# Pair 4 of the input projection between the steps of the sample indexer scores

## The chip, the cores and the metric

The kernel runs on one core of a Trainium2 chip. The metric is the device time of one execution in microseconds (us); several executions are taken and their median counts. The profile is of one execution, with its own time.

## What is computed

One layer of a hybrid decoder, for 256 prompt tokens and 8 x 4 = 32 sample tokens that share all weights. Cut to what matters here:

```python
p = rmsnorm(x) @ w_in                       # 2048 -> q, k, v, qi (16 heads x 64), ki, wi, conv and gate parts
# indexer of the sample tokens, over 2048 cached positions of each of 8 sequences (and 4 new ones)
s = relu(einsum('bthd,bsd->bths', qi, ki)) * 64**-0.5
score = einsum('bths,bth->bts', s, wi * 16**-0.5)
_, idx = top_k(score, 256)                  # per sample token
# attention over the 256 picked cache rows
out = sparse_attend(q, cache_k[page, off(idx)], cache_v[page, off(idx)])
x = x + (sigmoid(ga) * (out @ w_pa) + sigmoid(gb) * (conv @ w_pb)) @ w_o
x = x + relu(rmsnorm(x) @ w1)**2 @ w2       # 2048 -> 8192 -> 2048
```

## The kernel before, in words

All products with large weights are made in three fp32r matmuls each (high x high, high x low, low x high). `w_in` is cut into 44 pairs of 256 output columns; `win_half(p, half)` (L393) does half a pair, which is four *eighths*. An eighth is 12 matmuls of 288 columns and one `chunk_used` increment. Eighths are counted through: eighth u = 8 p + j, so pair 4 is eighths 32 to 39. For every eighth, SyncE loads the raw weights, ScalarE (ACT) makes the high part `VH` (`highs`, L881), and GpSimd (POOL) or, for some eighths from pair 16 on, VectorE (DVE) the low part `VL` (POOL's `lows`, L1706). `VH` and `VL` are rings of four, so ACT makes `VH` of eighth u when eighth u - 4 has been used, and the matmuls wait for `VL` (`low_done`). Pair p accumulates in PSUM banks 0 and 1 (even p) or 2 and 3 (odd p), and ACT's `evac` copies it out.

Every engine runs its own list of instructions, in the order that the program writes. Semaphores alone tie the lists together.

The helper `after` of `win_half` is called behind each eighth, and small work of PE is put there: while pairs 2 and 3 run, the prompt's indexer scores (`prompt_scores`, L551). The sample's indexer scores stand behind pair 3 as one block, with no eighth in it (L611 to L638). For sequence b:

- `turn_keys(b)` (L579): 8 transposes of cached index keys into banks 6 and 7; it waits for DVE's copies of two steps before (`kp_copied`).
- DVE's `keys(b)` (L1313) copies them to `kiP`.
- `scores(b)` (L591): 4 products of the queries with 512 keys each, into banks 0 and 1 for even b, 4 and 5 for odd b. ACT takes the ReLU of each bank (L988).
- `combine(b)` (L604): weights the 16 heads and sums them into banks 2 and 3, in 2 products. Each line of the profile counts these fp32 products twice.

Behind `combine(7)` ACT and DVE copy the scores to SBUF (L1345, `scomb_added`). PE waits for that, then does pairs 4 to 7. DVE goes on with the sample's top-k: 32 rounds of max, index and replace (L1361 to L1364), a merge of two halves up to `comb_ready` (L1381), and two steps of the prompt's own top-k (`prompt_top`, L1387). PE waits for `comb_ready` in `picked(0)`, behind the first eighth of pair 14 (L655 to L660), and spreads the positions. DVE works out the cache rows from these (L1396 to L1404, `rows_ready`).

POOL does `lows` of all eighths below 120, then waits for `rows_ready`:

```python
            lows(UNIT * KP)                      # KP = 15, UNIT = 8
            pool.wait_ge(S["rows_ready"], 1)
            for n in range(UNITS + RK):
                lows(UNIT * KP + n if n < RK else unit_end(n - RK) + 4)
                gather(n)
```

So each low part from eighth 120 on stands behind a gather of cache rows in POOL's list. DVE works on the gathered rows, one unit after another (L1433, L1438), and at n = 4 waits for PE's products of pair 16 (L684; DVE L1448).

Of the kernel before, what the change touches and what calls it, by code (L numbers as in the profile page):

```python
# [6 lines left out]
ACT = mybir.ActivationFunctionType  # L7
# [108 lines left out]
def build(nc, I, O):  # L116
    with ExitStack() as ctx:
# [267 lines left out]
        def _(pe):  # L385
# [165 lines left out]
            def prompt_scores(h):  # L551
                if h % 4 == 0:
                    pe.wait_ge(S["win_evac"], h // 4 + 1)
                if h == 0:
                    pe.wait_ge(S["kin_copied"], 2)
                    pe.wait_ge(S["wc_copied"], 1)
                else:
                    pe.wait_ge(S["pscore_relu"], h)
                for a, n in ((0, P), (P, SEQ)):
                    for e in range(2):  # L560
                        r = ID * e
                        m = pe.matmul(bank(5 - e, a, n), qiT[r:r + ID, h // 2, a % SEQ:a + P], kiT[r:r + ID, 0:n], start=True, stop=True)
                        if a:
                            m.then_inc(S["pscore_done"], 1)
# [14 lines left out]
            def turn_keys(b):  # L579
                pe.wait_ge(pages_in[b], 16)  # L580
                for c in range(2):
                    at = 2 * b + c
                    if at < 2:
                        pe.wait_ge(S["tab_copied"], H - 1 + at)
                    else:
                        pe.wait_ge(S["kp_copied"], at - 1)
                    for g in range(4):
                        m = transpose(bank(6 + c, g * P, P), rawk[b][:, 4 * c + g, :])
                    m.then_inc(S["kp_turned"], 1)

            def scores(b):  # L591

                pe.wait_ge(S["kp_copied"], 2 * b + 2)
                if b >= 2:
                    pe.wait_ge(S["sscore_relu"], 2 * b - 2)
                q = qs2[:, b].rearrange("p h t -> p (h t)")
                for c in range(2):
                    for e in range(2):
                        r, o = ID * e, ID * (e ^ c)
                        m = pe.matmul(PM[o:o + ID, 4 * (b % 2) + c, :], q[r:r + ID, :], kiP[r:r + ID, b % 2, 512 * c:512 * c + 512],  # L600
                                      start=True, stop=True)
                    m.then_inc(S["sscore_done"], 1)

            def combine(b):  # L604

                pe.wait_ge(S["sscore_relu"], 2 * b + 2)
                for c in range(2):
                    m = pe.matmul(PM[ID * c:ID * c + ID, 2 + c, :], Wc[:, b, :], rl[:, b % 2, c, :], start=(b == 0), stop=(b == DB - 1))
                m.then_inc(S["scomb_done"], 1)

            turn_keys(0)  # L611
            prompt_scores(12)
            prompt_scores(14)
            turn_keys(1)
            pe.wait_ge(S["wc_copied"], 1)
            pe.wait_ge(S["qs_copied"], 4)
            pe.wait_ge(S["pscore_relu"], IH)
            for b in range(DB):
                scores(b)
                if b == 0:  # L620
                    for i in range(DB):
                        m = pe.matmul(bank(3, DT * i, DT, ID), qs2[0:ID, i].rearrange("p h t -> p (h t)"),
                                      kiT[0:ID, SEQ + DT * i:SEQ + DT * i + DT], start=True, stop=True)
                    m.then_inc(S["snew_done"], 1)
                if b + 2 < DB:
                    turn_keys(b + 2)
                if b:
                    combine(b - 1)
            pe.wait_ge(S["snew_relu"], 1)
            for i in range(DB):  # L630
                m = pe.matmul(bank(3, ID, DT, NS), Wc[0:ID, i, 0:NS], rln[:, DT * i:DT * i + DT], start=(i == 0), stop=(i == DB - 1))
            m.then_inc(S["snew_done"], 1)
            combine(DB - 1)
            pe.wait_ge(S["consts_in"], 16)
            pe.wait_ge(S["ptf_ready"], 1)
            pe.wait_ge(S["kp_copied"], 2 * DB)
            pe.matmul(bank(5, 0, NPG), const("rall", NS), ptf[:], start=True, stop=True).then_inc(S["spread_done"], 1)
            pe.wait_ge(S["scomb_added"], 4)  # L638

            pairs(4, 8)  # L640
            win_half(8, 0)
            pe.wait_ge(S["win_evac"], 8)
            pe.wait_ge(S["ptw_read"], 1)
# [200 lines left out]
        def _(act):  # L844
# [137 lines left out]
                act.wait_ge(tabs[i], 32)  # L982
            for at in range(2 * DB):
                b, c = at // 2, at % 2
                act.wait_ge(S["sscore_done"], at + 1)
                if b >= 2:
                    act.wait_ge(S["scomb_done"], b - 1)
                act.activation(rl[:, b % 2, c, :], bank(4 * (b % 2) + c), ACT.Relu).then_inc(S["sscore_relu"], 1)  # L988
                if at == 1:
                    act.wait_ge(S["snew_done"], 1)  # L990
                    act.activation(rln, bank(3, 0, NS, ID), ACT.Relu).then_inc(S["snew_relu"], 1)
# [872 lines left out]
```

## Time and profile before

| | |
|---|---|
| median of 3 runs | 1791.46 us (1788.7 to 1793.67) |
| the profiled execution's own time | 1791.65 us |
| its span | 1789.9 us |
| PE, DVE, ACT, POOL busy | 1751.0, 1039.0, 690.1, 563.9 us |

Busy shares are means over stages. PE's matmuls overlap, so an eighth of 12 matmuls, each listed with some 0.3 us, starts a matmul every 0.13 us and takes 1.6 us. The timelines give starts in microseconds from the start of the span. An idle time stands in brackets with what ended it. PEclk is the granted TensorE clock as a share of the full one.

### The profile page before, as it was taken

To read this page: it belongs to the slowest core of one execution; us is meant where nothing else is said; L and a number is where in the kernel's file an instruction comes from. 1 tells how busy PE (TensorE), PEld (TensorE's weight loads), DVE (VectorE), ACT (ScalarE), POOL (GpSimd) and SP (SyncE) were. 2 spreads that over 40 slices of the span, in tenths; PEclk is the share of its full clock that TensorE was granted. 3 is DMA by queue.
4 is the path that set the end of the run, shared out by engine and by line. 5 is a ranking of instruction groups with operands and counts; after the bars stand their busy time and mean duration, and the time that the engine had idled before them with its cause. 6 is when DMAs were issued, how large, how long until landed. Compare 5 with 4: busy or idle time off the path is not lost.

```text
span 1789.9 us, 32474 instructions
## 1 busy us (share of the span) xinstructions
PE 1751.0 (98%) x13712; PEld 1701.0 (95%) x13712; DVE 1039.0 (58%) x1147; ACT 690.1 (39%) x845; POOL 563.9 (32%) x450
## 2 busy tenths in 40 slices
PE   9999999999999999999999999999999999999997
PEld 8859998999888999999999999999999999999996
DVE  4559997889989432255456554455444554455543
ACT  5534443543344555433333332233323332233332
POOL 3718778888866667400231000000000000000001
PEclk9999999999999999999999999999999999999998
DMA  6725457988879974654454444444444444444442
GB/s 211 239 66 156 153 166 256 349 296 295 306 263 316 337 275 152 209 182 159 167 187 156 165 164 165 164 165 163 166 163 165 164 164 165 164 165 164 163 165 100
DMA packets 73793, 348.53 MB, mean 195 GB/s; under 512 B 8978, under 2 KB 11154, under 8 KB 52660
## 3 DMA queue, kind: packets, MB, share of 16 engines
q1 hardware_dynamic: 50112, 268.00, 44.0%
q0 software_dynamic: 19584, 71.31, 11.4%
q10 hardware_dynamic: 3988, 7.66, 1.2%
q8 instruction: 81, 1.33, 0.3%
q14 instruction: 28, 0.23, 0.0%
HBM read 340.50 MB, written 6.44 MB: 194 GB/s over the span
## 4 chain that ended last, share of the span: by engine, by line
PE 86%; DVE 10%; POOL 2%; DMA 1%; issue 1%; ACT 0%; POOLq 0%; DVEq 0%; ACTq 0%
PE PM L426 19%; PE PM L428 19%; PE PM L427 19%; PE PM L406 8%; PE PM L408 7%; PE PM L407 7%; PE PM L391 2%; DVE lg L1438 2%; DVE kv L1433 2%; DVE VL L1428 2%; PE PM L783 1%; DMA kv<-cache_v,offs 1%; POOL VL L1712 1%; POOL kv L1726 1%; DVE sp L1498 1%
## 5 line engine op out<-in xcount | busy, mean ns | idle before, releaser
L849 ACT ACTIVATE WH<-wring 128x2048 fp32r<-128x2048 f32 (+1 forms) x163 | 307.3, 1885 | 679.9 <-PE PM L428 676.1
L1582 DVE TENSOR_TENSOR WL<-wring,WH 128x2048 fp32r<-128x2048 f32 x159 | 364.5, 2292 | 341.3 <-ACT WH L849 341.2
L406 PE MATMUL PM<-hH,VH 128*128 128x288 f32 x1408 | 428.9, 305 | 11.1 <-POOL VL L1712 6.9
L1712 POOL TENSOR_TENSOR VL<-wring,VH 128x512 fp32r<-128x512 f32 x292 | 383.4, 1320 | 163.5 <-ACT VH L849 147.8
L407 PE MATMUL PM<-hL,VH 128*128 128x288 f32 x1408 | 418.7, 297 | 0.0
L408 PE MATMUL PM<-hH,VL 128*128 128x288 f32 x1408 | 417.3, 296 | 0.0
L426 PE MATMUL PM<-XH,WH 128*128 128x288 f32 x1280 | 379.1, 296 | 1.5 <-DVE WL L1589 1.5
L426 PE MATMUL PM<-YH,WH 128*128 128x288 f32 x1280 | 379.4, 296 | 0.0
L427 PE MATMUL PM<-YL,WH 128*128 128x288 f32 x1280 | 377.6, 295 | 0.0
L427 PE MATMUL PM<-XL,WH 128*128 128x288 f32 x1280 | 377.6, 295 | 0.0
L428 PE MATMUL PM<-XH,WL 128*128 128x288 f32 x1280 | 376.3, 294 | 0.0
L428 PE MATMUL PM<-YH,WL 128*128 128x288 f32 x1280 | 376.3, 294 | 0.0
L849 ACT ACTIVATE VH<-wring 128x512 fp32r<-128x512 f32 x352 | 221.7, 631 | 336.7 <-PE PM L408 336.2
L406 PEld LDWEIGHTS PM<-hH,VH 128*128 128x128 f32 x1408 | 267.2, 190 | 24.6 <-POOL VL L1712 8.9
L408 PEld LDWEIGHTS PM<-hH,VL 128*128 128x128 f32 x1408 | 268.2, 190 | 0.0
L407 PEld LDWEIGHTS PM<-hL,VH 128*128 128x128 f32 x1408 | 267.6, 190 | 0.2
L1767 POOL TENSOR_SCALAR ysam<-ysam,small 32x1024 f32<-32x1024 f32 x2 | 6.2, 3122 | 824.1 <-DVE small L1688 824.1
L426 PEld LDWEIGHTS PM<-XH,WH 128*128 128x128 f32 x1280 | 239.8, 187 | 1.8 <-ACT G L926 1.7
L428 PEld LDWEIGHTS PM<-XH,WL 128*128 128x128 f32 x1280 | 241.0, 188 | 0.0
L428 PEld LDWEIGHTS PM<-YH,WL 128*128 128x128 f32 x1280 | 241.0, 188 | 0.0
L427 PEld LDWEIGHTS PM<-XL,WH 128*128 128x128 f32 x1280 | 240.2, 188 | 0.1
L427 PEld LDWEIGHTS PM<-YL,WH 128*128 128x128 f32 x1280 | 240.2, 188 | 0.0
(267 smaller groups left out, 1574.4 us busy)
## 6 DMA issues: line engine op xcount, KB each, us to landing
wring<-w_in SPq DMA_DIRECT2D x176, 512.0 KB, 4.6
wring<-w_mlp_in SPq DMA_DIRECT2D x64, 1024.0 KB, 5.2
wring<-w_mlp_out SPq DMA_DIRECT2D x64, 1024.0 KB, 5.2
wring<-w_o SPq DMA_DIRECT2D x16, 1024.0 KB, 5.2
wring<-w_pb SPq DMA_DIRECT2D x8, 1024.0 KB, 4.9
wring<-w_pa SPq DMA_DIRECT2D x8, 1024.0 KB
xT<-x_t SPq DMA_DIRECT2D x1, 2304.0 KB, 12.2
bias_scratch<-uv ACTq DMA_DIRECT2D x8, 192.0 KB, 4.6
```

Source lines behind the costliest of these rows:

```text
L391: return pe.transpose(out, in_, cp[0:n, 0:n])
L406: pe.matmul(out, vh, hH[:, k, :], start=(k == 0), stop=False)
L407: pe.matmul(out, vh, hL[:, k, :], start=False, stop=False)
L408: m = pe.matmul(out, vl, hH[:, k, :], start=False, stop=(k == KT - 1))
L426: pe.matmul(out, wh, rh[:, k0 + k, :], start=(first and k == 0), stop=False)
L427: pe.matmul(out, wh, rl_[:, k0 + k, :], start=False, stop=False)
L428: m = pe.matmul(out, wl, rh[:, k0 + k, :], start=False, stop=(last and k == CK - 1))
L849: return act.activation(out, in_, ACT.Copy, **kw)
L1428: dve.tensor_tensor(VL[:, u % 4], r, VH[:, u % 4], ALU.subtract).then_inc(S["vl_dve"], 1)
L1433: m = dve.tensor_tensor(by2, by2, PM[:, 6:8, :], ALU.mult)
L1582: dve.tensor_tensor(WL[:, i % 2], wring[:, i % 2], WH[:, i % 2], ALU.subtract).then_inc(S["wl_ready"], 1)
L1712: pool.tensor_tensor(VL[:, u % 4], r, VH[:, u % 4], ALU.subtract).then_inc(S["vl_pool"], 1)
```

## The change

The block of the sample scores is cut into four parts, and each is put behind one of the first four eighths of pair 4, by way of `after`. `turn_keys(0)` and `prompt_scores(12)` stay ahead of pair 4. Then:

- eighth 32, then `prompt_scores(14)` and `turn_keys(1)`
- eighth 33, then sequence 0's scores, `turn_keys(2)`, and the products with the new keys
- eighth 34, then the whole steps of sequences 1 to 7, and the new keys' weighting
- eighth 35, then `combine(7)` and the spread of the page table; then eighths 36 to 39

The wait for `scomb_added` now stands behind pair 4. Pair 4 needs banks 0 and 1, so all sample scores use banks 4 and 5, and scores of sequence b wait, for each of the two banks, for the ReLU of sequence b - 1. ACT makes `VH` of eighths 36, 37 and 38 between the ReLUs.

```diff
--- before.py
+++ after.py
@@ -591,13 +591,13 @@
             def scores(b):
 
                 pe.wait_ge(S["kp_copied"], 2 * b + 2)
-                if b >= 2:
-                    pe.wait_ge(S["sscore_relu"], 2 * b - 2)
                 q = qs2[:, b].rearrange("p h t -> p (h t)")
                 for c in range(2):
+                    if b:
+                        pe.wait_ge(S["sscore_relu"], 2 * b - 1 + c)
                     for e in range(2):
                         r, o = ID * e, ID * (e ^ c)
-                        m = pe.matmul(PM[o:o + ID, 4 * (b % 2) + c, :], q[r:r + ID, :], kiP[r:r + ID, b % 2, 512 * c:512 * c + 512],
+                        m = pe.matmul(PM[o:o + ID, 4 + c, :], q[r:r + ID, :], kiP[r:r + ID, b % 2, 512 * c:512 * c + 512],
                                       start=True, stop=True)
                     m.then_inc(S["sscore_done"], 1)
 
@@ -608,36 +608,47 @@
                     m = pe.matmul(PM[ID * c:ID * c + ID, 2 + c, :], Wc[:, b, :], rl[:, b % 2, c, :], start=(b == 0), stop=(b == DB - 1))
                 m.then_inc(S["scomb_done"], 1)
 
-            turn_keys(0)
-            prompt_scores(12)
-            prompt_scores(14)
-            turn_keys(1)
-            pe.wait_ge(S["wc_copied"], 1)
-            pe.wait_ge(S["qs_copied"], 4)
-            pe.wait_ge(S["pscore_relu"], IH)
-            for b in range(DB):
+            def ask(b):
+
                 scores(b)
-                if b == 0:
+                if b + 2 < DB:
+                    turn_keys(b + 2)
+                if b:
+                    combine(b - 1)
+
+            def samples(j):
+                if j == 0:
+                    prompt_scores(14)
+                    turn_keys(1)
+                    pe.wait_ge(S["wc_copied"], 1)
+                    pe.wait_ge(S["qs_copied"], 4)
+                    pe.wait_ge(S["pscore_relu"], IH)
+                elif j == 1:
+                    ask(0)
                     for i in range(DB):
                         m = pe.matmul(bank(3, DT * i, DT, ID), qs2[0:ID, i].rearrange("p h t -> p (h t)"),
                                       kiT[0:ID, SEQ + DT * i:SEQ + DT * i + DT], start=True, stop=True)
                     m.then_inc(S["snew_done"], 1)
-                if b + 2 < DB:
-                    turn_keys(b + 2)
-                if b:
-                    combine(b - 1)
-            pe.wait_ge(S["snew_relu"], 1)
-            for i in range(DB):
-                m = pe.matmul(bank(3, ID, DT, NS), Wc[0:ID, i, 0:NS], rln[:, DT * i:DT * i + DT], start=(i == 0), stop=(i == DB - 1))
-            m.then_inc(S["snew_done"], 1)
-            combine(DB - 1)
-            pe.wait_ge(S["consts_in"], 16)
-            pe.wait_ge(S["ptf_ready"], 1)
-            pe.wait_ge(S["kp_copied"], 2 * DB)
-            pe.matmul(bank(5, 0, NPG), const("rall", NS), ptf[:], start=True, stop=True).then_inc(S["spread_done"], 1)
+                elif j == 2:
+                    for b in range(1, DB):
+                        ask(b)
+                    pe.wait_ge(S["snew_relu"], 1)
+                    for i in range(DB):
+                        m = pe.matmul(bank(3, ID, DT, NS), Wc[0:ID, i, 0:NS], rln[:, DT * i:DT * i + DT], start=(i == 0), stop=(i == DB - 1))
+                    m.then_inc(S["snew_done"], 1)
+                else:
+                    combine(DB - 1)
+                    pe.wait_ge(S["consts_in"], 16)
+                    pe.wait_ge(S["ptf_ready"], 1)
+                    pe.wait_ge(S["kp_copied"], 2 * DB)
+                    pe.matmul(bank(5, 0, NPG), const("rall", NS), ptf[:], start=True, stop=True).then_inc(S["spread_done"], 1)
+
+            turn_keys(0)
+            prompt_scores(12)
+            win_half(4, 0, samples)
+            win_half(4, 1)
             pe.wait_ge(S["scomb_added"], 4)
-
-            pairs(4, 8)
+            pairs(5, 8)
             win_half(8, 0)
             pe.wait_ge(S["win_evac"], 8)
             pe.wait_ge(S["ptw_read"], 1)
@@ -982,10 +993,12 @@
                 act.wait_ge(tabs[i], 32)
             for at in range(2 * DB):
                 b, c = at // 2, at % 2
+                if at in (2, 4, 6):
+                    highs(UNIT * 4 + 4 + at // 2)
                 act.wait_ge(S["sscore_done"], at + 1)
                 if b >= 2:
                     act.wait_ge(S["scomb_done"], b - 1)
-                act.activation(rl[:, b % 2, c, :], bank(4 * (b % 2) + c), ACT.Relu).then_inc(S["sscore_relu"], 1)
+                act.activation(rl[:, b % 2, c, :], bank(4 + c), ACT.Relu).then_inc(S["sscore_relu"], 1)
                 if at == 1:
                     act.wait_ge(S["snew_done"], 1)
                     act.activation(rln, bank(3, 0, NS, ID), ACT.Relu).then_inc(S["snew_relu"], 1)
```

## Rows read from the trace of the kernel before

**Rows 1.** The page's first part: engine, busy us (share of the span), instructions.

```profile
PE 1751.0 (98%) x13712; PEld 1701.0 (95%) x13712; DVE 1039.0 (58%) x1147; ACT 690.1 (39%) x845; POOL 563.9 (32%) x450
```

**Rows 2.** Stretches: busy us of PE, PEld, DVE, ACT, POOL; granted clock, DMA share, GB/s.

```profile
96.00:132.00 36.00, 31.61 (x225) 15.15 (x224) 19.57 (x43) 13.13 (x26) 2.24 (x2) 0.95 0.11 30
132.00:262.00 130.00, 130.00 (x967) 128.46 (x966) 126.38 (x176) 55.75 (x90) 100.66 (x79) 1.00 0.52 162
410.00:420.00 10.00, 6.69 (x30) 6.46 (x30) 9.86 (x10) 1.26 (x2) 7.84 (x7) 0.66 0.67 222
```

**Rows 3.** PE's timeline: start, us, engine, line, operation, count, [idle before <-releaser].

```profile
88.78 0.40 PE L406 MATMUL PM<-hH,VH 128*128 128x288 f32 x1
...
92.17 0.93 PE L562 MATMUL PM<-kiT,G 64*128 64x128 f32 x8
...
98.83 0.93 PE L562 MATMUL PM<-kiT,G 64*128 64x128 f32 x8 [0.47 <-ACT G L926]
100.71 0.93 PE L562 MATMUL PM<-kiT,G 64*128 64x128 f32 x8 [0.95 <-ACT rlp L959]
...
103.67 1.04 PE L622 MATMUL PM<-kiT,qs 64*64 64x4 f32 x16
106.06 1.91 PE L391 MATMUL PM<-cp,kv 128*128 128x128 f32 x8 [1.34 <-DVE zB L1319]
...
109.69 1.09 PE L391 MATMUL PM<-cp,kv 128*128 128x128 f32 x8
...
112.74 1.09 PE L391 MATMUL PM<-cp,G 128*128 128x128 f32 x8
...
127.98 0.66 PE L631 MATMUL PM<-uv,zB 64*32 64x4 f32 x16
128.58 1.08 PE L608 MATMUL PM<-uv,zB 128*64 128x512 f32 x4
...
131.50 0.40 PE L406 MATMUL PM<-hH,VH 128*128 128x288 f32 x1 [1.52 <-DVE small L1350]
```

**Rows 4.** ACT's timeline, a ReLU pair of the sample scores.

```profile
112.84 1.09 ACT L988 ACTIVATE uv<-PM 128x512 f32<-128x512 f32 x2 [1.96 <-PE PM L600]
```

**Rows 5.** POOL's timeline, the low part of pair 4's fourth eighth.

```profile
97.28 1.27 POOL L1712 TENSOR_TENSOR VL<-wring,VH 128x512 fp32r<-128x512 f32 x1 [0.32 <-ACT VH L849]
```

**Rows 6.** DVE's timeline, around the sample top-k.

```profile
129.77 1.41 DVE L1345 COPY scw<-PM 32x512 f32<-32x512 f32 x2 [5.90 <-PE PM L608]
...
260.93 0.41 DVE L1381 TENSOR_TENSOR comb<-PM,scw 32x256 f32<-32x256 f32 x1
...
265.53 0.23 DVE L1396 TENSOR_SCALAR small<-PM 128x64 f32<-128x64 f32 x1 [0.91 <-PE PM L659]
```

**Rows 7.** PE's timeline at the picked positions.

```profile
264.25 1.18 PE L659 MATMUL PM<-comb,cp 32*128 32x64 f32 x8
265.35 0.40 PE L406 MATMUL PM<-hH,VH 128*128 128x288 f32 x1
```

**Rows 8.** POOL's timeline where its gathers begin.

```profile
268.02 4.62 POOL L1712 TENSOR_TENSOR VL<-wring,VH 128x512 fp32r<-128x512 f32 x3 [1.62 <-ACT VH L849]
272.96 0.95 POOL L1726 DMA_INDIRECT kv<-cache_k,offs  x1 [0.32 <-DVE offs L1404]
...
280.56 2.83 POOL L1726 DMA_INDIRECT kv<-cache_k,offs  x1 [0.16 <-issue]
```

**Rows 9.** DVE's timeline, the compare beside those gathers and the next wait on PE.

```profile
278.62 3.94 DVE L1417 TENSOR_TENSOR scw<-dist,cp 128x2048 f32<-128x2048 f32 x1
...
303.40 0.16 DVE L1448 TENSOR_SCALAR newsel<-PM 128x1 f32<-128x1 f32 x1 [8.33 <-PE PM L684]
```

**Rows 10.** PE's timeline, two of its waits for POOL behind the gathers.

```profile
284.73 0.40 PE L406 MATMUL PM<-hH,VH 128*128 128x288 f32 x1 [2.42 <-POOL VL L1712]
...
293.25 0.40 PE L406 MATMUL PM<-hH,VH 128*128 128x288 f32 x1 [0.22 <-POOL VL L1712]
```

**Rows 11.** PE's timeline, a longer wait for POOL in the unit loop.

```profile
414.08 0.61 PE L406 MATMUL PM<-hH,VH 128*128 128x288 f32 x1 [3.31 <-POOL VL L1712]
```

## The prediction

> **What bounds the kernel now.** I read the page's busy shares first. PE is busy for 1751.0 of 1789.9 us [rows 1], so the natural guess is that every microsecond saved on PE is a microsecond of the end. The stretches correct that. In 96:132, the block of sample scores, PE is busy for only 31.61 of 36 us, at a clock of 0.95. In 132:262 PE has no idle time, but DVE is busy for 126.38 of 130 us too [rows 2]: two engines run side by side there, and which of them arrives last at their meeting has to be read from the timelines. The reader is to look in these for brackets, which are idle time with its releaser.
>
> PE's timeline of the block shows four losses [rows 3]. PE waits 0.95 us for the ReLUs of prompt scores ahead of 100.71, 1.34 us for DVE's key copy ahead of 106.06, and 1.52 us for DVE's score copies ahead of 131.50. The fourth is clock: behind the wait of 1.34 us, transposes take 1.91 us where the same eight take 1.09 us at 109.69. From 106.06 to 109.69 PE does two thirds of a step (transposes, scores) in 3.63 us. A whole step of three equal parts takes 3.05 us (109.69 to 112.74), two thirds 2.03, so the half clock costs 1.6 us. The sum of what could be filled is 0.95 + 1.34 + 1.6 + 1.52 = 5.4 us.
>
> DVE's timeline shows the other side. DVE waits 5.90 us for PE's last combine and starts on the copies at 129.77. From there its list is a chain of dependent steps up to the merge that ends at 260.93 + 0.41 = 261.34 (`comb_ready`) [rows 6]. PE comes to the picked positions at 264.25 [rows 7]: DVE has 2.9 us in hand at this meeting. DVE fills them with its prompt top-k until 264.62, then waits 0.91 us for PE and goes on at 265.53 [rows 6]. POOL's first gather at 272.96 is released by DVE's cache rows [rows 8], and PE waits for POOL's low parts behind the gathers, 2.42 us at 284.73 and 0.22 us at 293.25 [rows 10].
>
> **The change, PE's side.** Without a break PE starts 967 matmuls in 130 us [rows 2], 0.134 us each, so an eighth of 12 takes 1.6 us. Two eighths between small work take 92.17 - 88.78 = 3.4 us [rows 3], so entry and exit together cost 0.2, and a single eighth costs 1.8 us. PE's list from `prompt_scores(12)` on becomes: eighth 32 covers the wait of 0.95, eighths 32 and 33 put `turn_keys(2)` at 98.83 + 0.9 + 1.8 + 0.9 + 1.0 + 1.8 + 1.0 = 106.2 (scores, eighth, scores, transposes, eighth, sequence 0's scores), which is past the 106.06 at which DVE's copy is there. The order of the new keys' products (1.04 us at 103.67) and `turn_keys(2)` is swapped, which costs nothing by that sum. With no long idle stretch I take the clock as full, as it is in all other steps of the block. The 1.52 us go behind pair 4, where DVE's two copies of together 1.41 us have four eighths, 6.4 us, to be done in. PE gains 5.4 less four more pairs of seams, 4 x 0.2 = 0.8, so 4.6 us. The low parts of the four eighths are ready: POOL finishes the fourth at 98.55 [rows 5]. If these weren't hidden, each would cost 1.3 us, its duration.
>
> **The change, two banks.** A pair of ReLUs starts at 112.84, which is 1.12 us behind its scores' start (two thirds of a step behind 109.69), and ends 2.2 us behind it, the first 1.65 us behind it [rows 3, 4]. The next scores of that bank come a step later, 3.05 us, and in the last step, which has no transposes, 2.03 and 2.54 us for the two banks. All are later than the ReLUs; the narrowest slack is 0.3 us. ACT's three high parts stand between ReLU pairs, where ACT waits 1.96 us each time; a high part of 0.63 us fits. Cost nothing; from the other side, if each of the seven steps waited for one high part, 7 x 0.6 = 4 us.
>
> **The change, DVE's side.** This decides. `combine(7)` now stands behind four eighths that it did not stand behind before. It ends later by 4 x 1.80 = 7.2 less the losses filled ahead of it, 0.95 + 1.34 + 1.6 = 3.9: by 3.3 us. DVE's whole chain starts 3.3 us later, and `comb_ready` comes at 261.34 + 3.3 = 264.6. PE would be there at 264.25 - 4.6 = 259.65 and waits 5.0 us. PE's gain is gone at one blow: it goes on at 264.7, 0.45 us later than before. DVE does its prompt steps until 264.62 + 3.3 = 267.9, by which PE's positions (1.1 us, 2.2 at half clock) are there, so it no longer waits 0.91 us: 267.9 against 265.53, 2.4 us later. The cache rows, and with them POOL's first gather, are 2.4 us later. PE then meets POOL. The eighth that starts at 284.73 is number 123, ten behind the one at 265.35 [rows 7]. Without a wait PE would start it at 265.35 + 0.45 + 10 x 1.61 = 281.9, but POOL's low part moves with the gathers, and with it the start, to 287.1. So PE is 2.4 us late there too and at 293.25. Behind that nothing resynchronises: DVE waits 8.33 us for PE at 303.40 [rows 9], so it starts its units 2.4 us later, and PE, DVE, POOL all carry the shift to the end. I find no place where one of them has work that did not shift.
>
> **Bounds of the shift.** A wait of 5.0 us is longer than any shown. Behind 3.31 us at 414.08 the first matmul takes 0.61 instead of 0.40 us [rows 11], and 410:420 has a clock of 0.66, 6.8 us of ten at the half level [rows 2]; behind 1.34 us the half level lasted 3.6 us. So PE probably loses 1.8 to 3.4 us behind the positions. That is covered by the 5.2 us between 281.9 and 287.1. It can still delay POOL: its last low parts end at 272.64, 0.32 us ahead of the gather [rows 8]; moved by 0.45 + 3.4 they end at 276.5, 1.4 us later than the cache rows (275.1). Upper end 2.4 + 1.4 = 3.8 us. The fourth gather, though, takes 2.83 us instead of 0.95, and ends at 283.39, 0.8 us behind DVE's compare of 278.62 + 3.94 [rows 8, 9]; if the compare holds it, POOL's lateness is absorbed there. I take 2.4. Lower end: if the drop at 106 stays in spite of the filling, DVE is 1.6 us later still and PE gains less, which is again on the upper side; if the seams cost nothing, 1.6.
>
> The Trainium skill speaks against the pinning: "SBUF — State Buffer", section "Who interferes with whom", says that a DVE instruction with two SBUF inputs contends with a GpSimd instruction that reads SBUF and not with one that only writes it, and infers that descriptor generation needs the write side. By that rule the gather would pass the compare, and the sum would be 2.4 to 3.8; by the row of 2.83 us it is 2.4.
>
> **Rivals.** First, the gain holds: PE is the bound, DVE has room, and the end is 4.6 us earlier, 1791.46 - 4.6 = 1786.9. For it: PE's share of 98%, and no PE idle time in 132:262. Against it: the 2.9 us of slack are less than the 3.3 by which DVE starts later, and the later waits for POOL hang on DVE. It needs DVE's list to be no chain, or a later wait of DVE for PE that sets the end.
>
> Second, clearly slower, by the clock: the wait of 5.0 us at 259.65 is followed by the low level, and the waits ahead of the eighth of 287.1 by another fall, which lies behind POOL's last gate at 295.6 and is not covered. It decides as soon as the second low stretch reaches past 295.6. Price 1.8 to 3.4 us on 2.4 to 3.8: 1795.7 to 1798.7. For it: a fall stood behind 1.34 us of idle time. Against it: behind 2.42 us the matmul at 284.73 takes 0.40 us, and so does the one at 293.25 [rows 10], against 0.61 at the low level.
>
> The skill, in "TensorE: Matmul & The Clock Gate", section "HAM oscillation — how this bites in real kernels", says that a long wait between bursts sends the engine back to half clock and that each burst then starts slowly. The fall behind 3.31 us agrees; by this rule the new wait of 5.0 us does the same, and by the rows its cover holds.
>
> Third, two banks are too few and every step waits, 4 us on PE and on DVE's start: 1791.5 + 2.4 + 4 = 1797.9.
>
> **Numbers.** The profiled execution took 1791.65 us, 1.75 more than its span of 1789.9 and 0.2 more than the median of the runs. The shift put on the median gives 1791.46 + 2.4 = 1793.9; I say 1794. The chances: this account 0.68, the gain holds 0.08, the clock 0.17, the banks 0.07. What can be told from no change is about 0.3%, 5.4 us, so below 1786.1 or above 1796.8. Faster by that needs the first rival and more, 0.04; slower is half of the clock's cases, most of the banks', and a tail of the forecast, 0.16; the same is 0.80. The forecast's own range is 1791 to 1797. For 8 in 10, with the runs before spread over 5 us, I give 1788.5 to 1798.5.
>
> **What would show it.** Right: no PE bracket of 1.34 or 1.52 us near 106 and 131; a full clock in the steps; `combine(7)` 3 us later; eighth 36 without a wait; a new wait of PE of some 5 us ahead of L659 with DVE's L1381 as releaser; DVE's 0.91 us ahead of L1396 gone; the first gather at 275 to 276; the eighth of 284.73 near 287; everything behind 293 shifted by the same amount. Wrong: no wait at L659, or PE brackets of half a microsecond ahead of each L600, or DVE's units starting earlier than at 303.4.

## The result: slower by 0.47%, beyond the upper end of the range

The changed kernel takes 1798.87 us (median of 6 runs, 1798.39 to 1803.62), the kernel before 1790.88 us (6 runs). The ratio is 1.0047, 95% interval [1.0035, 1.0059]. The forecast was 1794, the range 1788.5 to 1798.5. The shift has the sign of the forecast and about three times its size (8.0 us by the medians, 2.4 forecast). The wait that the forecast named is there, but the first gather is not released by what it named. The case "within 0.3%", which had 0.80, is not what came.

Spans and busy times of the profiled execution (1798.39 us) come first; the line answers to [rows 1].

```profile
PE 1754.3 (98%) x13712; PEld 1703.9 (95%) x13712; DVE 1041.4 (58%) x1147; ACT 690.2 (38%) x845; POOL 564.6 (31%) x450
```

The stretches of the changed kernel answer to [rows 2]: busy time of PE, PEld, DVE, ACT, POOL, then clock, DMA share and GB/s.

```profile
96.00:132.00 36.00, 35.39 (x264) 19.97 (x263) 18.41 (x36) 14.22 (x28) 6.11 (x5) 1.00 0.13 41
132.00:262.00 130.00, 127.84 (x944) 125.13 (x942) 125.23 (x167) 56.26 (x91) 100.40 (x78) 1.00 0.53 163
266.00:275.00 9.00, 8.51 (x39) 8.39 (x40) 8.46 (x23) 1.21 (x2) 1.55 (x1) 0.56 0.01 3
310.00:320.00 10.00, 10.00 (x58) 10.00 (x58) 9.42 (x9) 1.92 (x4) 5.58 (x5) 0.66 0.74 250
```

The block of the sample scores is what it was meant to be: PE is busy for 35.39 of 36 us at full clock. But 132:262 now has idle time on PE, and 266:275 runs at a clock of 0.56. PE's timeline answers to [rows 3, 7, 10, 11].

```profile
105.34 1.09 PE L600 MATMUL PM<-zB,qs 64*64 64x512 f32 x8
106.36 1.09 PE L391 MATMUL PM<-cp,kv 128*128 128x128 f32 x8
107.38 1.09 PE L629 MATMUL PM<-kiT,qs 64*64 64x4 f32 x16
...
110.19 1.09 PE L600 MATMUL PM<-zB,qs 64*64 64x512 f32 x8
...
132.10 1.08 PE L608 MATMUL PM<-uv,zB 128*64 128x512 f32 x4
133.11 0.39 PE L644 MATMUL PM<-ptf,cp 32*128 32x16 f32 x2
...
266.49 1.96 PE L670 MATMUL PM<-comb,cp 32*128 32x64 f32 x8 [6.65 <-DVE comb L1394]
268.38 0.61 PE L406 MATMUL PM<-hH,VH 128*128 128x288 f32 x1
...
290.52 0.40 PE L406 MATMUL PM<-hH,VH 128*128 128x288 f32 x1 [0.56 <-POOL VL L1725]
...
299.03 0.40 PE L406 MATMUL PM<-hH,VH 128*128 128x288 f32 x1 [0.21 <-POOL VL L1725]
...
421.44 0.61 PE L406 MATMUL PM<-hH,VH 128*128 128x288 f32 x1 [3.31 <-POOL VL L1725]
```

None of the three waits of [rows 3] behind 98.83 is left, and no transposes at half clock. `combine(7)` starts at 132.10 instead of 128.58, 3.5 us later. PE then waits 6.65 us for DVE ahead of L670 (before: L659), and its products take 1.96 us instead of 1.18. At 299.03 PE is 5.8 us late against 293.25, at 421.44 it is 7.4 us late against 414.08.

DVE's timeline answers to [rows 6, 9], POOL's to [rows 8].

```profile
133.30 1.41 DVE L1358 COPY scw<-PM 32x512 f32<-32x512 f32 x2 [7.89 <-PE PM L608]
134.63 1.25 DVE L1362 TENSOR_SCALAR small<-cp 32x4 f32<-32x4 f32 x1
135.92 0.15 DVE L1363 TENSOR_TENSOR small<-PM,cp 32x4 f32<-32x4 f32 x1
136.10 1.29 DVE L1365 TENSOR_TENSOR small<-small 32x4 f32<-32x4 f32 x1
...
137.90 1.21 DVE L1374 MAX8 scw<-scw 64x8 f32<-64x1026 f32 x1
...
266.02 0.41 DVE L1394 TENSOR_TENSOR comb<-PM,scw 32x256 f32<-32x256 f32 x1
...
269.75 0.22 DVE L1409 TENSOR_SCALAR small<-PM 128x64 f32<-128x64 f32 x1
...
274.14 0.23 DVE L1416 SCALAR_TENSOR_TENSOR small<-dist,small 128x64 f32<-128x64 f32 x1
274.40 0.20 DVE L1417 CAST offs<-small 128x64 uint32<-128x64 f32 x1
...
281.21 2.29 DVE L1430 TENSOR_TENSOR scw<-dist,cp 128x2048 f32<-128x2048 f32 x1
```
```profile
134.57 1.29 POOL L1725 TENSOR_TENSOR VL<-wring,VH 128x512 fp32r<-128x512 f32 x1 [17.26 <-ACT VH L860]
136.09 1.29 POOL L1725 TENSOR_TENSOR VL<-wring,VH 128x512 fp32r<-128x512 f32 x1 [0.23 <-ACT VH L860]
...
275.14 3.58 POOL L1725 TENSOR_TENSOR VL<-wring,VH 128x512 fp32r<-128x512 f32 x2 [1.15 <-ACT VH L860]
278.87 0.95 POOL L1739 DMA_INDIRECT kv<-cache_k,offs  x1 [0.15 <-issue]
...
281.30 3.03 POOL L1739 DMA_INDIRECT kv<-cache_k,offs  x1 [0.16 <-issue]
...
288.21 0.95 POOL L1739 DMA_INDIRECT kv<-cache_k,offs  x1 [0.16 <-issue]
```

For comparison, the same short steps of DVE in the kernel before, POOL's first low part behind the block, and DVE's last two steps to the cache rows:

```profile
131.11 0.15 DVE L1349 TENSOR_SCALAR small<-cp 32x4 f32<-32x4 f32 x1
131.29 0.15 DVE L1350 TENSOR_TENSOR small<-PM,cp 32x4 f32<-32x4 f32 x1
131.48 0.15 DVE L1352 TENSOR_TENSOR small<-small 32x4 f32<-32x4 f32 x1
```
```profile
134.16 1.29 POOL L1712 TENSOR_TENSOR VL<-wring,VH 128x512 fp32r<-128x512 f32 x1 [35.61 <-ACT VH L849]
```
```profile
270.25 1.20 DVE L1403 SCALAR_TENSOR_TENSOR small<-dist,small 128x64 f32<-128x64 f32 x1
271.49 1.19 DVE L1404 CAST offs<-small 128x64 uint32<-128x64 f32 x1
```

Three things stand here that the forecast did not have.

- Two steps of DVE behind the score copies take 1.25 and 1.29 us, where the one between them takes 0.15 us as all three did; both lie under a low part of POOL (134.57 and 136.09, 1.29 us each).
- DVE's cache rows are there at 274.60, but the first gather goes out at 278.87: POOL was still at two low parts, 275.14 to 278.72. Its bracket says "issue", not DVE.
- DVE does L1409 4.2 us later than L1396 before, but its cache rows come only 1.9 us later (274.60 against 272.68). In the kernel before, the last two steps took 1.20 and 1.19 us beside POOL's low parts; here POOL is idle then and they take 0.23 and 0.20 us. So of the first gather's 5.9 us, DVE's lateness makes 1.9.

### The profile page after: what moved, and what is told of

Read it like the earlier page. It is cut to its first block, busy times and chain, and to the rows that moved or that the text cites. A ratio compares the mean times of both kernels' runs of the same rounds, so it can differ in the third digit from the quotient of the medians.

```text
span 1796.6 us, 32475 instructions
## 1 busy us (share of the span) xinstructions
PE 1754.3 (98%) x13712; PEld 1703.9 (95%) x13712; DVE 1041.4 (58%) x1147; ACT 690.2 (38%) x845; POOL 564.6 (31%) x450
## 4 chain that ended last, share of the span: by engine, by line
PE 80%; DVE 16%; POOL 2%; DMA 1%; issue 1%; ACT 1%; POOLq 0%; ACTq 0%; DVEq 0%
PE PM L426 19%; PE PM L428 19%; PE PM L427 19%; PE PM L406 6%; PE PM L408 5%; PE PM L407 5%; DVE ix L1375 2%; DVE scw L1377 2%; DVE scw L1374 2%; PE PM L391 2%; DVE lg L1451 2%; DVE kv L1446 2%; DVE VL L1441 1%; PE PM L794 1%; POOL VL L1725 1%
## 5 line engine op out<-in xcount | busy, mean ns | idle before, releaser
L1725 POOL TENSOR_TENSOR VL<-wring,VH 128x512 fp32r<-128x512 f32 x292 | 383.2, 1319 | 172.2 <-ACT VH L860 155.4
```

The costliest lines, as they stand in the source:

```text
L1725: pool.tensor_tensor(VL[:, u % 4], r, VH[:, u % 4], ALU.subtract).then_inc(S["vl_pool"], 1)
```

## The experiments

Profiles differ by up to 3.4 us ahead of the changed part; in 16:45 the granted clock was 0.88 in some (before, after) and 0.76 in others (e1, e3). So times are given here from the start of `prompt_scores(12)` in the same profile (98.83 before, 98.87 after). L659, L1396 and L684 are the lines of the kernel before; the same instructions have other line numbers in the changed ones. Ratios are against runs of the kernel before on the same chip.

| | score copies | top-k starts | L659 | L1396 | first gather | L684 | ratio, 95% interval |
|---|---|---|---|---|---|---|---|
| before | 30.9 | 33.3 | 165.4 | 166.7 | 174.1 | 203.5 | 1 |
| after | 34.4 | 39.0 | 167.6 | 170.9 | 180.0 | 209.2 | 1.0047 [1.0035, 1.0059] |
| e1_picked_late | 34.4 | 39.0 | 167.7 | 170.9 | 176.0 | 205.3 | 1.0021 [1.0011, 1.0031] |
| e2_keep_warm | 34.5 | 39.1 | 167.7 | 170.9 | 178.1 | 207.4 | 1.0022 [1.0012, 1.0031] |
| e3_two_eighths | 30.8 | 33.1 | 162.4 | 165.7 | 172.8 | 202.4 | 1.0006 [0.9997, 1.0016] |
| e4_two_banks | 31.2 | 33.5 | 165.6 | 166.9 | 174.4 | 203.7 | 1.0007 [0.9997, 1.0017] |
| e5_quiet_start | 34.4 | 36.8 | 167.3 | 169.3 | 174.4 | 203.8 | 1.0004 [0.9993, 1.0014] |
| e6_two_tops_later | 30.8 | 33.1 | 162.4 | 163.6 | 169.8 | 199.4 | 0.9985 [0.9975, 0.9996] |
| e7_dve_delayed | 34.3 | 36.7 | 171.0 | 172.3 | 179.7 | 209.2 | 1.0047 [1.0031, 1.0062] |
| e8_tops_later | 30.7 | 33.1 | 165.2 | 166.4 | 173.9 | 203.2 | 0.9998 [0.9988, 1.0007] |
| e9_chain_late_3 | 31.0 | 40.1 | 169.0 | 172.2 | 179.8 | 210.0 | 1.0040 [1.0028, 1.0053] |
| e10_chain_late_8 | 30.9 | 52.9 | 181.0 | 184.3 | 193.4 | 222.7 | 1.0107 [1.0090, 1.0124] |
| e11_quiet_only | 34.4 | 36.8 | 166.0 | 169.3 | 176.8 | 206.8 | 1.0026 [1.0015, 1.0036] |
| e12_four_tops_later | 34.5 | 36.8 | 167.3 | 168.5 | 173.7 | 203.1 | 1.0002 [0.9992, 1.0012] |

Two readings hold for all rows. From the first gather to L684 every profile takes 29.2 to 30.1 us: what the first gather is late by, L684 is late by, within a microsecond. Behind L684 chance comes in. The clock falls beside the small products of L688 in some profiles and not in others, and from L688 to the next transposes of `kT` it takes 6.9 us with no fall (e5, e9, e11), 8.4 us with 3.4 us at the low level (before, e2, e4, e8), and 10.0 us with 6.8 us (the rest). No edit was made to change that. The profiled execution of e9 took 1796.05 us and four of its six took 1799.05 to 1800.38, so it seems to differ between executions of one kernel too; no second profile of a kernel shows it. Up to 3 us of a difference between two rows can be this fall.

**The wait and the clock: e1 and e2.**

```diff
-            win_half(KP - 1, 0, picked)
-            win_half(KP - 1, 1)
+            win_half(KP - 1, 0)
+            win_half(KP - 1, 1, picked)
```

> The changed kernel, with the products at the picked positions (L670) moved from behind the first eighth of pair 14 to behind its fifth, four eighths later (6.4 us of PE work ahead of the wait). Theory A (the wait of 6.65 us ahead of L670 lowers TensorE's clock to half until 274.8, so eighths 113 to 119, POOL's low parts behind them and POOL's first gather come late): the wait shrinks to under 1 us, no low clock in 262:276, the first gather comes at 275 to 277 instead of 278.9, and the kernel takes 1795 to 1797 us. Theory B (only DVE's own chain, 5.1 us late at L1394, sets the end): the first gather stays at 278.9 and the time at 1799 us. Prediction's account with only sizes off: as A.

Measured: 1796.23 us. PE does its four eighths ahead of the wait, which is 0.28 us instead of 6.65; 262:276 is at full clock (in the changed kernel the low level ends at 274.0, not at 274.8); the first gather waits for DVE's rows again and comes 4.0 us earlier. By the ratios that is 0.26% or 4.7 us of the loss of 0.47%. PE and POOL in e1:

```profile
269.92 1.17 PE L670 MATMUL PM<-comb,cp 32*128 32x64 f32 x8 [0.28 <-DVE comb L1394]
...
280.99 0.58 PE L406 MATMUL PM<-hH,VH 128*128 128x288 f32 x1 [4.91 <-POOL VL L1725]
```
```profile
278.30 0.95 POOL L1739 DMA_INDIRECT kv<-cache_k,offs  x1 [8.18 <-DVE offs L1417]
```

PE's lead is still worth nothing: it is idle for 4.91 us ahead of 280.99, at the first low part behind a gather. The clock falls there instead (6.8 us at the low level in 279:287), but PE is paced by the gathers in that stretch, and L684 follows the first gather by 29.3 us as elsewhere.

```diff
                 if j == 0:
+                    pe.wait_ge(S["win_evac"], KP - 1)
+                    for i in range(26):
+                        pe.matmul(bank(2, 0, P), ones[:], ones[:], start=True, stop=True)
                     pe.wait_ge(S["comb_ready"], 1)
```

> The changed kernel, with 26 idle products of the ones tile (128 columns, fp32, about 6 us) ahead of the wait for comb_ready, so that PE is busy while it waits. Nothing else moves. Theory A (the clock after the wait): full clock in 266:276, L670 at 266.5 as before the edit, eighth 113 to 119 in 11.3 us instead of 15, first gather at 275 to 276.5, time 1794.5 to 1796.5 us. Theory B (DVE's lateness alone): L670 at 266.5 and 1799 us all the same.

Measured: 1795.9 us. L659 starts at the same time as in the changed kernel, and the stretch 262:276 has these values (PE busy, clock, DMA share, GB/s):

```profile
262.00:276.00 14.00, 13.15 (x104) 1.00 0.22 74
```

The clock behind the wait is what this edit changes, and its ratio is that of e1 (1.0022 and 1.0021). The first gather gains less (1.9 us) since POOL now works beside DVE's steps to the rows: DVE's 128x1024 products take 2.26 and 2.20 us there, 1.23 in the changed kernel. The shorter fall behind L684 (3.4 us instead of 6.8 at the low level in the profile) may be the rest of the gain. The theory of the wait and the clock holds, that of DVE's lateness alone does not: with L659 as late as in the changed kernel, the gather is earlier.

**The short steps under POOL: e5 and e11.**

```diff
+            act.wait_ge(S["ptw_read"], 1)
             for p in range(4, 8):
                 evac(p, qT[:, 2 * (p - 4):2 * (p - 4) + 2, :])
```

ACT's high parts from eighth 39 on, and with them POOL's low parts, now wait until DVE has done its short steps. In e5 this stands beside the edit of e1, in e11 alone.

> The changed kernel with the picked positions behind the fifth eighth of pair 14 (as in e1_picked_late), and ACT's next high parts (eighth 39 on) held back until DVE's short steps behind combine(7) are done (ACT waits for ptw_read). Theory C (in the changed kernel POOL's low parts at 134.57 and 136.09 hold DVE's short steps of 0.15 us for 1.25 and 1.29 us, so the top-k starts 2.2 us later than combine(7) makes it): those two steps take 0.15 us again, the top-k starts 3.6 us behind the start of the score copies' line less 1.4 (2.4 us behind it instead of 4.6), comb_ready is 2.2 us earlier relative to the score copies, and the kernel is 1 to 2.2 us faster than e1_picked_late (1796.2). Rival: the short steps are slow for another reason and nothing moves; 1796 us.

> The changed kernel, with only ACT's high parts from eighth 39 on held back until DVE's short steps are done; the picked positions stay behind the first eighth of pair 14. With the changed kernel, e1_picked_late and e5_quiet_start it makes a two by two of the two causes. Short steps 0.15 us each, comb_ready 1.6 to 2.2 us earlier than in the changed kernel, but a wait of about 5 us at L659 remains, the clock falls, POOL's low parts are late as they were. If the causes add: 1.5 to 2.2 us faster than the changed kernel, 1797 us. If the clock alone sets the first gather: no faster than by the shorter wait, 1797 to 1799 us.

Measured: 1791.84 us (e5) and 1795.31 us (e11). DVE and POOL in e5:

```profile
134.48 1.41 DVE L1359 COPY scw<-PM 32x512 f32<-32x512 f32 x2 [7.90 <-PE PM L608]
135.82 0.15 DVE L1363 TENSOR_SCALAR small<-cp 32x4 f32<-32x4 f32 x1
136.00 0.15 DVE L1364 TENSOR_TENSOR small<-PM,cp 32x4 f32<-32x4 f32 x1
136.19 0.15 DVE L1366 TENSOR_TENSOR small<-small 32x4 f32<-32x4 f32 x1
...
136.85 1.21 DVE L1375 MAX8 scw<-scw 64x8 f32<-64x1026 f32 x1
```
```profile
137.68 2.56 POOL L1726 TENSOR_TENSOR VL<-wring,VH 128x512 fp32r<-128x512 f32 x2 [19.18 <-ACT VH L860]
```

POOL's next low part starts behind the short steps, and all three take 0.15 us: the top-k starts 2.2 us earlier. The four kernels make a two by two. Above the kernel before stand 0.47% (neither repair), 0.21% (picked late), 0.26% (quiet start), and 0.04% (both). Taken alone the repairs bring 0.26 and 0.21%, together 0.43%; each of the four has an interval of some 0.1% on either side, so a difference of two is known to about 0.15%, and that the causes add is in keeping with it, no more. For the quiet start the profiles show 2.4 us (changed kernel to e11) and 1.5 us (e1 to e5) at L684, where the ratios say 3.8 and 3.0 us; the profiles of e5 and e11 are among those with no fall behind L684.

e11 keeps a wait and a low clock, and it meets the forecast's own conditions: a chain that starts as late as `combine(7)` makes it, and a wait of 5.06 us where the forecast had 5.0. PE and POOL in e11:

```profile
265.25 1.96 PE L670 MATMUL PM<-comb,cp 32*128 32x64 f32 x8 [5.06 <-DVE comb L1395]
```
```profile
276.02 1.76 POOL L1740 DMA_INDIRECT kv<-cache_k,offs  x1
```

Its cache rows are there at 175.1 in the table's time, 1.3 us later than in the kernel before (173.9). Its first gather comes 2.7 us later, again right behind POOL's last low part (its end is at 275.88) and not behind the rows (274.33), and 2.4 us behind e5's.

**The delay of combine(7): e3, e12 and e6.**

```diff
                     m.then_inc(S["snew_done"], 1)
-                elif j == 2:
                     for b in range(1, DB):
                         ask(b)
...
-                else:
                     combine(DB - 1)
```

ACT's third high part between the ReLUs (`at == 6`) goes too, since it needs eighth 34, which now stands behind `combine(7)`.

> The changed kernel with only eighths 32 and 33 ahead of combine(7); eighths 34 and 35 follow behind combine(7) and the spread. Theory A plus the delay of combine(7): combine(7) ends at 129.6 to 130 instead of 133.1, the top-k starts about 3 to 5 us earlier than in the changed kernel, PE's lead at the picked positions is the same 4.6 us over the kernel before, so the wait there is 1.7 to 4 us and may or may not lower the clock; time 1790 to 1794 us. Rival C (not the order of combine(7) but the low parts that POOL now makes while DVE does its short steps set the delay): the top-k still starts 2 us later than combine(7) alone would make it, 1793 to 1796 us. Rival B: as far as DVE starts earlier, the time falls by the same amount.

Measured: 1792.92 us. `combine(7)` is 3.7 us earlier than in the changed kernel, the short steps fall clear of POOL, and PE waits 1.88 us at L659. The loss shrinks to 0.06%, which can't be told from none.

```diff
-            for i in range(2):
-                prompt_top(i)
...
                 if n == 4:
+                    for i in range(2):
+                        prompt_top(i)
                     dve.wait_ge(S["spread_done"], 3)
```

e6 adds this to e3, with `picked` at `j == 1`; e12 adds it to e5; e8 to the kernel before.

> Eighths 32 and 33 between the steps, 34 and 35 behind combine(7) (as in e3_two_eighths); the picked positions behind the second eighth of pair 14; DVE's two prompt top-k steps (3.3 us) moved from behind comb_ready into the place where it waits for PE at n = 4 of the units. Theory (DVE's path comb_ready, positions, cache rows, first gather sets the shift once PE is early): L1396 1.2 us behind L659's start instead of 3.3 us behind it, the first gather 1.5 to 2.5 us earlier than in e3_two_eighths relative to prompt_scores(12), 1789.5 to 1791.5 us, which is 1 to 2.5 us faster than the kernel before. Rival (PE's own work sets the end between 160 and 303 too): the time is e3_two_eighths's, 1792.9 us. Other rival: another fall of the clock behind a longer wait at the eighth of the fourth gather eats it.

> All four eighths between the steps as in the change, with every repair: ACT held back until the short steps are done, the picked positions behind the fifth eighth of pair 14, DVE's two prompt top-k steps in its wait at n = 4. Against e6_two_tops_later it asks what the 3.5 us cost by which combine(7) ends later behind two more eighths. If DVE's chain is the path: 2 to 4 us slower than e6_two_tops_later (1789.6), 1791.5 to 1793.5 us. If it isn't: the same as e6_two_tops_later.

> The kernel before, with only DVE's two prompt top-k steps moved from behind comb_ready to the units' wait at n = 4. PE comes to L659 at 264.25 as before, so DVE now waits there for PE and L1396 starts at 265.5 as before: no change in time, 1792 us within 0.1%. It is the control for e6_two_tops_later. Rival (the two steps are on the path in the kernel before as well): 1 to 3 us faster.

Measured: 1789.6 us (e6), 1793.33 us (e12), 1791.59 us (e8). e6 is faster than both kernels. In e6 DVE waits for PE again, and POOL's first gather follows the rows:

```profile
262.18 0.41 DVE L1392 TENSOR_TENSOR comb<-PM,scw 32x256 f32<-32x256 f32 x1
263.86 0.23 DVE L1404 TENSOR_SCALAR small<-PM 128x64 f32<-128x64 f32 x1 [1.26 <-PE PM L668]
```
```profile
266.42 3.01 POOL L1722 TENSOR_TENSOR VL<-wring,VH 128x512 fp32r<-128x512 f32 x2 [1.97 <-ACT VH L858]
270.01 0.95 POOL L1736 DMA_INDIRECT kv<-cache_k,offs  x1 [0.58 <-DVE offs L1412]
```

e8 shows that the move alone gives nothing while PE is the later one at L659. e12 against e6 shows the delay of `combine(7)` with no held short step and no fall of the clock at L659 in either: 3.7 us at the score copies and 3.7 us at `comb_ready`. Behind that the two differ in more. The picked positions stand three eighths later in e12, and DVE waits 2.52 us for them instead of 1.26; its steps from L1396 to the cache rows take 4.9 us instead of 5.9. The first gather is 3.9 us later by the sum of these, and the time by 0.17%, 3.0 us (the two intervals overlap a little).

**Two banks: e4.**

```diff
-                        m = pe.matmul(PM[o:o + ID, 4 * (b % 2) + c, :], q[r:r + ID, :], kiP[r:r + ID, b % 2, 512 * c:512 * c + 512],
+                        m = pe.matmul(PM[o:o + ID, 4 + c, :], q[r:r + ID, :], kiP[r:r + ID, b % 2, 512 * c:512 * c + 512],
```

> The kernel before, with its order of work untouched, but all sample scores in banks 4 and 5 and the scores of sequence b waiting, bank by bank, for the ReLUs of sequence b - 1. Theory: nothing waits for that, PE's steps keep 3.05 us, and the time is the kernel before's 1791 us within 0.1%. Rival D (two banks are too few): each step takes up to 0.6 us more, 1793 to 1795 us.

Measured: 1793.06 us, ratio 1.0007, not told from 1. The steps keep 3.05 us (L600 at 113.21, 116.26, 119.31). Only in the last step, which has no transposes, does L600 take 1.31 us instead of 1.09 (127.44), and all behind it is 0.2 us later, L684 too. Rival D, which had up to 0.6 us in each step, falls.

**The chain made late by other work: e7, e9, e10.**

```diff
             dve.wait_ge(S["scomb_done"], DB)
+            for i in range(9):
+                step(dve.tensor_scalar(lps[0][:], const("causal"), -1.0, -NEG, ALU.add, ALU.mult))
```

> The kernel before, with nine more DVE steps (128x384 tensor_scalar into a free tile, together about 3.4 us) between combine(7) and the score copies. PE's order is untouched. This asks the prediction's central step alone: what 3.4 us on DVE's chain cost when PE is not early. By it PE waits 0.5 to 1 us at L659 and keeps its clock, L1396 and the first gather come 2.4 us later, and the time is 1793.5 to 1795 us (ratio 1.001 to 1.002). If DVE is not on the path: 1792 us. If the lateness alone explains the change's 8 us: 1798 us or more.

Measured: 1800.39 us. The edit was badly placed: PE waits for the score copies ahead of pair 4, so it was held as well, 5.08 us instead of 1.52, and came to L659 5.6 us later. It tells nothing on DVE's chain alone. e9 and e10 put the steps behind `ptw_read`:

```diff
             dve.tensor_tensor(ptw[:], bank(5, 0, NPG), const("iota"), ALU.subtract).then_inc(S["ptw_read"], 1)
+            for i in range(9):                 # e10: 21
+                step(dve.tensor_scalar(lps[0][64:128, :], const("rs")[64:128, 0:3 * P], -1.0, 2.0, ALU.add, ALU.mult))
```

> The kernel before, with nine DVE steps (128x384 in form, on 64 partitions, 0.38 us each, 3.4 us if nothing holds them) put behind the release of scomb_added and ptw_read and ahead of the top-k. e7_dve_delayed held PE up as well, because PE waits for scomb_added ahead of pair 4; here PE's order and its times up to L659 stay as before, so this is the prediction's central step by itself. By it: comb_ready at 264.7 relative to the kernel before's clock, PE waits about 0.5 us at L659, L1396 and the first gather come 2.4 us later, time 1794 us (ratio 1.0013). Theory E (what starts 3.4 us late ends 8 us late by whatever way): 1799 us.

> As e9_chain_late_3 with 21 steps, 8 us if nothing holds them, so PE waits about 5 us at L659, as it does in the changed kernel, with none of the change in it. Theory A (the clock): the clock falls to half in the wait and stays there for 3 to 8 us behind it, POOL's low parts 117 to 119 come later than the cache rows, and the first gather comes 9 us later than in the kernel before although the rows come 5 to 7 us later; 1800 to 1803 us. Without a fall of the clock the gather follows the rows, 7.3 us later, 1799 us.

Measured: 1799.34 us (e9) and 1811.94 us (e10). The delays were not those asked for. The nine steps take 6.62 us in e9, 0.74 each, where the nine of e7, of twice the partitions, took 0.39 each: in e9 three low parts of POOL run beside them, in e7 none. The top-k starts 6.8 and 19.5 us late. Neither theory's number can be read off, but the structure can. In e9 L1396 is 5.5 us late, the 6.4 us of `comb_ready` less the 0.9 of idle time; the forecast took its own 2.4 from 3.3 in the same way. In e10, which has nothing of the change in it, PE waits and POOL is late in the same way. Its PE timeline, a stretch of PE (busy, clock, DMA share, GB/s), and its POOL timeline:

```profile
281.41 1.96 PE L659 MATMUL PM<-comb,cp 32*128 32x64 f32 x8 [15.56 <-DVE comb L1383]
```
```profile
281.00:290.00 9.00, 8.59 (x39) 0.56 0.04 6
```
```profile
290.06 3.56 POOL L1714 TENSOR_TENSOR VL<-wring,VH 128x512 fp32r<-128x512 f32 x2 [1.16 <-ACT VH L849]
293.77 0.95 POOL L1728 DMA_INDIRECT kv<-cache_k,offs  x1
...
296.22 3.03 POOL L1728 DMA_INDIRECT kv<-cache_k,offs  x1 [0.16 <-issue]
```

L1396 is 17.6 us late and the first gather 19.3 us. The rows are there at 289.5; the gather goes out at 293.77, right behind POOL's two low parts.

## Why the prediction was wrong in size

**PE's side** was right. PE came to the picked positions at 259.84 instead of 264.25 [rows 7], 4.4 us earlier, forecast 4.6; the clock stayed full in the block. The two banks cost 0.2 us where the forecast had nothing: in the last step L600 takes 1.31 us instead of 1.09, at 127.48 here and at 127.44 in e4. The slack of 0.3 us that the forecast read there was not enough.

**The delay of combine(7)** was right, 3.5 us for 3.3, and so was the rule that it goes through to `comb_ready` (3.7 and 3.7 us, e12 against e6).

**The step "DVE's whole chain starts 3.3 us later"** failed. The top-k started 5.7 us later, since the steps behind the copies took 2.2 us more under POOL's low parts, and `comb_ready` came 5.1 us later (the cast of L1378 took 0.72 us instead of 1.39). So PE waited 6.65 us instead of 5.0. In the kernel before POOL makes no low part between 98.55 and 134.16, because PE has finished no eighth, and DVE's short steps are done by then. With eighths between the steps ACT and POOL go on at once behind `combine(7)`, just there. The forecast counted the eighths' own low parts as ready, and did not ask what the ones made next would lie beside. e5 and e11 show this cause: `comb_ready` is 1.6 us earlier in e11 than in the changed kernel, the first gather 3.2 us, the time 0.21%.

**The term "it can still delay POOL", taken at nothing,** failed, and it is the largest. The forecast had this path, with an upper end of 1.4 us behind the cache rows, and took none of it. Measured: POOL's low part 119, which hangs on PE's eighth 115, ended at 278.72, 4.1 us behind the rows. Of the 2.7 us above the upper end, 1.8 are PE going on at 266.49 instead of 264.7, which is the held short steps again; 0.5 are the rows, which came at 274.60 instead of 275.1; and 0.4 are left for the clock and for POOL's two last low parts, which took 1.79 us each instead of 1.29. At a clock of 0.56, 7.9 of the nine microseconds from 266 on are at the low level; without the 0.5 ahead of the first product that is 7.4 us with work, a loss of 3.7, forecast at most 3.4. PE itself was covered, as forecast: it waited 1.75 us for POOL at 285.69. e1 shows the term by taking it away: without wait and fall the first gather goes out behind the rows, 1.9 us later than before. e11 shows its size under the forecast's own wait: the rows 1.3 us later, the first gather 2.7. That is near the 2.4 of the forecast, but by another path; the agreement would have been luck.

**The rows.** "2.4 us later" at L1396 was 4.2 us, and at the cache rows 1.9. The forecast carried the delay of L1396 through to the rows unchanged. It did not see that two of DVE's steps there were held by POOL in the kernel before, and would be free once POOL is late.

**The pinning** by the fourth gather, for which the forecast took nothing on POOL, failed with it. The compare lay beside the second gather this time, 3.03 us at 281.30, and the fourth took 0.95 us. Both long gathers end 0.83 us behind the compare's end (283.39 and 282.56 before, 284.33 and 283.50 after), so the compare does hold a gather. The Trainium skill, "SBUF — State Buffer", section "Who interferes with whom", which would let it pass, does not fit these two rows; but the hold absorbs no lateness larger than itself.

**The rival "clearly slower, by the clock"** named 1795.7 to 1798.7 with a second fall behind 295.6. The first fall alone did it, by way of POOL. Behind the small products of L684 a fall came too, as in the kernel before, but longer. The clock of 0.66 in 310:320 is 6.8 us at the low level, against 3.4 us in the kernel before; the difference costs 1.6 us (10.0 against 8.4 us from L688 to the transposes) and is the step from 5.8 to 7.4 us late. It isn't settled what lengthened it, and it may be the execution and not the kernel: e5, e9 and e11 have no fall there at all, the others have one of 3.4 or 6.8 us, and no run was made to test it.

## What to carry to other kernels

Filling idle time of the busiest engine pays only as far as its next meeting with another chain. Find that meeting first, and put ahead of the instruction that starts the other chain only as much filler as its own waits hold: two eighths ahead of `combine(7)` and two behind it (e3, e6) kept PE's gain and cost DVE nothing. That alone gave no time (e3); it took the later place of two other pieces to be faster than the kernel before, by 0.15% (e6). A wait made longer is not just idle time given back. It can drop TensorE's clock, and what is then late is not only TensorE but each engine that is paced by its instructions. And where an engine starts work earlier, look at which short steps of others it now lies beside.

## What the runs showed of the hardware

DVE steps were longer beside a POOL product of 1.29 us: 32x4 steps of 0.15 us took 1.25 and 1.29 us (changed kernel), 128x64 steps of 0.23 and 0.20 us took 1.20 and 1.19 us (kernel before), and a 128x1024 product of 1.23 us took 2.26 us (e2). Not each one was: the product at 267.74 in the kernel before, which had begun 0.28 us ahead of POOL's low part, took its 1.22 us.

The low clock lasted for 3.6 us of work behind 1.34 us of idle time in the kernel before, for 5.4 us behind 5.06 us in e11, for 7.4 us behind 6.65 us in the changed one, and for 7.5 us behind 15.56 us (e10). Ahead of the same products, a wait of 1.88 us (e3) was followed by 3.4 us at the low level (266:270 at a clock of 0.57), and one of 0.28 us (e1, e6) by none. The same idle time need not bring the same clock: behind 2.42 us the matmul at 284.73 in the kernel before ran at the full clock, and the one at 286.52 in e3 took 0.61 us at the low level. And the clock fell with no idle time too, behind the small products of L684 and L688 (307:311 of the kernel before, PE busy throughout, at 0.57).
